# Gated layers: each head's mean of squares from high and low parts in the short format, the norm's steps two k-steps later

## The reference

```python
def rmsnorm(x, g):
    y = xf * lax.rsqrt(jnp.mean(xf * xf, axis=-1, keepdims=True) + EPS)
    return y * g
# gla_mixer: q, k, v, r from h @ w_in; o from the chunked recurrence
# y = (rmsnorm(o, head_norm) * silu(r)) @ w_out
```

## Time and profile before

| | us |
|---|---|
| median of 3 runs | 2536.77 (2536.25 to 2537.08) |
| the profiled execution | 2536.17 |
| its span | 2534.4 |
| PE busy | 2516.1 (99%) |
| DVE busy | 1747.4 (69%) |
| ACT busy | 1206.0 (48%) |
| POOL busy | 169.1 (7%) |

### The profile page before, as it was taken

How to read it: one execution, slowest core, us unless ns; L and a number is a source line. 1 busy time by engine, 2 the same in 40 slices (tenths; PEclk the granted TensorE clock), 3 DMA queues, 4 the chain that set the end, 5 groups by cost and what they waited for, 6 DMA issues and landing times.

```text
span 2534.4 us, 48129 instructions
## 1 busy us (share of the span) xinstructions
PE 2516.1 (99%) x19925; PEld 2451.5 (97%) x19925; DVE 1747.4 (69%) x2578; ACT 1206.0 (48%) x1822; POOL 169.1 (7%) x180
## 2 busy tenths in 40 slices
PE   8999999999999999999999999999999999999998
PEld 8999999999988899999998899999999999999998
DVE  6555994984555599489557557948955565984973
ACT  5454651543555565245245545524534544642543
POOL 1101000001000010000122210000011101000001
PEclk9999999999999999999999999999999999999999
DMA  4222333332433233333222233332323223333332
GB/s 120 71 78 84 100 102 91 100 96 78 120 97 109 74 108 96 97 95 96 85 68 76 70 91 88 102 102 84 97 81 88 72 70 90 109 88 93 106 89 78
DMA packets 443890, 230.68 MB, mean 91 GB/s; under 512 B 17092, under 2 KB 440736, under 8 KB 443696
## 3 DMA queue, kind: packets, MB, share of 16 engines
q1 hardware_dynamic: 442048, 226.90, 31.2%
q10 hardware_dynamic: 1200, 0.59, 0.1%
q0 software_dynamic: 448, 0.45, 0.1%
HBM read 219.03 MB, written 8.87 MB: 90 GB/s over the span
## 4 chain that ended last, share of the span: by engine, by line
PE 96%; DVE 2%; ACT 1%; issue 1%; DMA 0%; SPq 0%; ACTq 0%; DVEq 0%
PE slot L2378 32%; PE slot L2421 21%; PE aux L2885 6%; PE aux L2880 6%; PE aux L2882 6%; PE slot L2885 5%; PE slot L2880 5%; PE slot L2882 5%; PE aux L2337 2%; PE aux L2783 1%; PE aux L2546 1%; PE aux L2789 1%; PE aux L2695 1%; PE aux L2633 1%; PE aux L2561 1%
## 5 line engine op out<-in xcount | busy, mean ns | idle before, releaser
L765 ACT ACTIVATE w_hi<-raw 128x1024 fp32r<-128x1024 f32 (+3 forms) x208 | 241.1, 1159 | 275.3 <-PE slot L2421 136.7
L2378 PE MATMUL slot<-xg_hi,w_hi 128*128 128x272 f32 x1664 | 361.4, 298 | 2.5 <-DVE w_lo L1462 1.5
L2378 PE MATMUL slot<-xg_lo,w_hi 128*128 128x272 f32 x1664 | 343.7, 288 | 0.0
L2378 PE MATMUL slot<-xg_hi,w_lo 128*128 128x272 f32 x1664 | 343.6, 288 | 0.0
L1462 DVE TENSOR_TENSOR w_lo<-raw,w_hi 128x1024 fp32r<-128x1024 f32 (+4 forms) x208 | 284.2, 1366 | 68.8 <-ACT w_hi L765 66.8
L2378 PEld LDWEIGHTS slot<-xg_hi,w_hi 128*128 128x128 f32 x1664 | 260.5, 189 | 14.2 <-issue 7.8
L2378 PEld LDWEIGHTS slot<-xg_lo,w_hi 128*128 128x128 f32 x1664 | 261.3, 188 | 0.0
L2378 PEld LDWEIGHTS slot<-xg_hi,w_lo 128*128 128x128 f32 x1664 | 260.3, 189 | 0.0
L2982 POOL TENSOR_TENSOR sq_sum<-sq_sum,sq_x 128x544 f32<-128x544 f32 x48 | 67.9, 1414 | 1609.8 <-ACT sq_x L783 1609.5
L2097 DVE TENSOR_TENSOR ffn_y<-slot,rstd 128x544 f32<-128x544 f32 x56 | 40.6, 725 | 193.9 <-PE slot L2421 177.7
L2421 PE MATMUL slot<-h_hi,w_hi 128*128 128x272 f32 x1078 | 150.0, 287 | 0.0
(11 more groups left out here) (406 smaller groups left out, 5757.4 us busy)
## 6 DMA issues: line engine op xcount, KB each, us to landing
raw<-in_l_ffn_w_out_dram SPq DMA_DIRECT2D x64, 704.0 KB, 4.7
raw<-in_l_ffn_w_in_dram SPq DMA_DIRECT2D x52, 512.0 KB, 5.0
raw<-in_l_gla_w_in_dram SPq DMA_DIRECT2D x47, 512.0 KB, 3.9
ffn_raw_b<-in_l_ffn_w_in_dram SPq DMA_DIRECT2D x88, 256.0 KB, 3.4
ffn_raw_b<-in_l_ffn_w_in_dram SPq DMA_DIRECT2D x44, 512.0 KB, 5.2
raw<-in_l_ffn_w_in_dram SPq DMA_DIRECT2D x72, 256.0 KB, 3.4
raw<-in_l_att_w_qkv_dram SPq DMA_DIRECT2D x24, 512.0 KB, 3.8
raw<-in_l_lru_w_in_dram SPq DMA_DIRECT2D x24, 512.0 KB, 3.9
```

The source lines that it names most:

```text
L765: act.activation(w_hi[par][:, 0:kt, :], raw[par][:, 0:kt, :], ACT.Copy).then_inc(s_hi, 1)
L2378: ins = pe.matmul((slot[par] if bank is None else bank)[:, hf, 0:HALF], w[par][:, k, :], a[:, k0 + k, hf * HALF:(hf + 1) * HALF], start=(k ...
```

## The change

- The sum of squares is split as the weights are: ACT copies it to fp32r (`square_hi`, step 64), DVE subtracts the copy from it (`square_lo`, step 65). The two parts lie where `inv` and `sq1` lie.
- The mean is four fp32r matmuls with a constant matrix of 1/256 in fp32r, which the format holds exactly: 512 columns and 32 columns of the high part, then the same of the low part, summed in PSUM. PE waits for the low part.
- The mean moves from step 66 to 68, the root from 67 to 69, the inverse from 69 to 71, the norm products from 70 and 71 to 72 and 73.
- The constant is written by DVE into a start-up tile and copied once to fp32r by ACT at the start.
- Some semaphores are merged (abs and exp share one, cumulative sum and middle share one); the waits and their order stay.

```diff
-        mean_h = sb("mean_h", [P, P])
+        mean_hr = sb("mean_h", [P, P], F32R)
...
             act.wait_ge(s_vk, 3)
+            act.activation(mean_hr[:, :], ST["mean_f"][:, :], ACT.Copy)
             act.activation(rms5[:, 0:1], eps[:, 0:1], ACT.Sqrt)
...
+                def square_hi(h):
+
+                    q = h + 4 * gl
+                    act.wait_ge(s_hp, q + 1)
+                    act.wait_ge(s_on, 2 * q)
+                    act.activation(GL["sq_hi"][:, :], GL["sq0"][:, :], ACT.Copy).then_inc(s_sqh, 1)
...
-                    if n == 67:
+                    if n == 64:
+                        square_hi(h)
+                    if n == 69:
                         head_rms(h)
...
+                def square_lo(h):
+
+                    q = h + 4 * gl
+                    dve.wait_ge(s_sqh, q + 1)
+                    dve.tensor_tensor(GL["sq_lo"][:, :], GL["sq0"][:, :], GL["sq_hi"][:, :].bitcast(F32),
+                                      ALU.subtract).then_inc(s_sql, 1)
...
-                    if n == 69:
+                    if n == 65:
+                        square_lo(h)
+                    if n == 71:
                         head_inv(h)
-                    if n in (70, 71):
-                        o_norm(h, n - 70)
+                    if n in (72, 73):
+                        o_norm(h, n - 72)
...
                 def mean_sq(h):
 
-                    pe.wait_ge(s_hp, h + 4 * gl + 1)
-                    pe.matmul(A0[:, :], mean_h[:, :], GL["sq0"][:, 0:SEQ], start=True, stop=True)
-                    pe.matmul(A1[:, 0:DEC_SEQ], mean_h[:, :], GL["sq0"][:, SEQ:TOK], start=True, stop=True).then_inc(s_hst, 1)
+                    pe.wait_ge(s_sql, h + 4 * gl + 1)
+                    for part, src in enumerate((GL["sq_hi"], GL["sq_lo"])):
+                        pe.matmul(A0[:, :], mean_hr[:, :], src[:, 0:SEQ], start=(part == 0), stop=(part == 1))
+                        ins = pe.matmul(A1[:, 0:DEC_SEQ], mean_hr[:, :], src[:, SEQ:TOK], start=(part == 0), stop=(part == 1))
+                    ins.then_inc(s_hst, 1)
...
-                    if n == 66:
+                    if n == 68:
                         mean_sq(h)
```

More of the change, by code:

```diff
@@ L243, in make_start @@
                         tri_f=a("tri_f", [P, P]), behind=a("start_behind_gate", [P, 48 * P]), gain_rows=a("gain_rows", [P, P]),
-                        squares=a("x_rows_sq", [P, QT + 1, D_MODEL]), xs=a("x_sample_gain", [P, XT, DEC_SEQ]))
+                        squares=a("x_rows_sq", [P, QT + 1, D_MODEL]), xs=a("x_sample_gain", [P, XT, DEC_SEQ]),
+                        mean_f=a("mean_f", [P, P]))
         def make_ffn(a):
@@ L259, in make_gla @@
         def make_gla(a):
+            with ExitStack() as c:
+                sb("gla_in_front", [P, 11 * TOK], F32, c)
+                sq_hi = sb("gla_sq_hi", [P, TOK], F32R, c)
+                sb("gla_sq0_there", [P, TOK], F32, c)
+                sq_lo = sb("gla_sq_lo", [P, TOK], F32R, c)
             b = {n: a("gla_" + n, [P, TOK]) for n in
                  ("q", "k", "z", "mn", "ez", "b", "eb", "enb", "ekd", "ke", "kd", "inv", "sq0", "sq1")}
-            b["yv"] = b["q"]
+            b["yv"], b["sq_hi"], b["sq_lo"] = b["q"], sq_hi, sq_lo
             b["wb_in"], b["low_in"] = b["sq0"][0:GATE_ROWS, 0:GLA_HEADS * GLA_DK], b["sq1"][0:GATE_ROWS, :]
@@ L334, in encoder_step @@
         s_raw = [sem(f"raw_in{s}") for s in range(2)]
-        s_mid, s_bm = sem("gla_mid"), sem("gla_b_from_mid")
+        s_bm = sem("gla_b_from_mid")
         s_hi, s_lo, s_mm, s_free = sem("w_hi"), sem("w_lo"), sem("block_done"), sem("block_read")
@@ L342, in encoder_step @@
         s_out7, s_dcp, s_tact, s_tdve, s_xd = sem("seven_summed"), sem("seven_d_b_copied"), sem("t_act"), sem("t_dve"), sem("x_from_scaled")
-        s_wb, s_gm, s_z, s_abs, s_exp, s_ln, s_mn, s_g, s_b, s_e, s_df, s_ekd = (sem("gla_" + n) for n in (
-            "gate_b_in", "gate_mm", "z", "abs", "exp", "ln", "min", "g", "cumsum", "exps", "diff", "exp_kd"))
+        s_wb, s_gm, s_z, s_ez, s_ln, s_mn, s_g, s_b, s_e, s_df, s_ekd = (sem("gla_" + n) for n in (
+            "gate_b_in", "gate_mm", "z", "abs_then_exp", "ln", "min", "g", "cumsum_then_mid", "exps", "diff", "exp_kd"))
         s_qe, s_ke, s_kd, s_vtm, s_vte, s_kdm, s_kde, s_atm, s_ate, s_um, s_s, s_om, s_oe, s_sil = (sem("gla_" + n) for n in (
@@ L371, in encoder_step @@
             "mm", "x", "square", "x_gain", "squares_summed", "mean_mm", "rms", "inv_rms", "turned"))
-        s_hp = sem("head_square")
+        s_hp, s_sqh, s_sql = sem("head_square"), sem("head_square_hi"), sem("head_square_lo")
         def one3(t, n, a, b, parts=slice(0, P)):
@@ L861, in gate @@
                     act.wait_ge(s_g, q)
[L862 to L865, removed]
+                    act.activation(GL["ez"][:, :], GL["z"][:, :], ACT.Abs).then_inc(s_ez, 1)
+                    act.wait_ge(s_ez, 2 * q + 1)
+                    act.activation(GL["ez"][:, :], GL["ez"][:, :], ACT.Exp, scale=-1.0).then_inc(s_ez, 1)
+                    act.wait_ge(s_ez, 2 * q + 2)
                     act.activation(GL["ez"][:, :], GL["ez"][:, :], ACT.Ln, bias=1.0).then_inc(s_ln, 1)
@@ L1447, in _ @@
             dve.memset(row_sq[:, :], 1.0)
-            dve.memset(mean_h[:, :], 1.0 / GLA_DV)
+            dve.memset(ST["mean_f"][:, :], 1.0 / GLA_DV)
             dve.memset(chunk_go[:, :], 1.0).then_inc(s_vk, 1)
@@ L1630, in cumsum @@
                     dve.tensor_tensor_scan(GL["b"][:, :], chunk_go[:, :], GL["mn"][:, :], 0.0, ALU.mult, ALU.add).then_inc(s_b, 1)
-                    dve.wait_ge(s_b, q + 1)
+                    dve.wait_ge(s_b, 2 * q + 1)
                     spans = GL["b"][:, 0:SEQ].rearrange("p (c n) -> p c n", n=P)
@@ L1635, in cumsum @@
                     dve.tensor_tensor(b_end[:, 0:NCHUNK - 1], GL["b"][:, P - 1:SEQ - P:P], GL["b"][:, P + CHUNK - 1:SEQ:P],
-                                      ALU.add).then_inc(s_mid, 1)
-                    dve.wait_ge(s_mid, q + 1)
+                                      ALU.add).then_inc(s_b, 1)
+                    dve.wait_ge(s_b, 2 * q + 2)
                     dve.tensor_tensor(spans[:, :, 0:CHUNK], spans[:, :, 0:CHUNK],
```

## The result

The changed kernel takes 2539.78 us (median of 20 runs, 2538.01 to 2541.65) against 2536.46 for the kernel before on the same chips (20 runs, 2535.75 to 2537.13): a ratio of 1.0013, 95% interval 1.0007 to 1.0019. That is 3.3 us slower, within 0.2%. The profiled execution took 2539.79, its span is 2538.1. The runs of the changed kernel spread over 3.6 us, those of before over 1.4.

What follows compares the result with a forecast made beforehand. PE was taken as the bound, with 96% of the chain. Terms of −1.9 (mean), +0.3 (waits in heads 0 to 2) and +3.4 (head 3) gave +1.8 us on 2536.77: 2538.6, range 2534.2 to 2541.2.

Steps and rivals of the forecast that it cites:

- part 1: Mean's matmuls on PE: 0.68 us a head instead of 1.00, or 1.09 in head 3; 2.7 us gain if nothing waits.
- Rival E: Mean's matmuls: four weight loads lie open, 0.92 us a head, gain 0.08 instead of 0.32; 2540.0 us, chance 0.05.
- part 2: Squares' copy on ACT and subtract on DVE: 16 instructions, about 11 us, off the bounding engine; no cost.
- part 3: Heads 0 to 2, turning the next head's v waits for ACT's root: 0.05 us for each of six heads, 0.3 us.
- Rival D: Heads 0 to 2: turning v waits for a whole table load, up to 1.28 us a head; 2546.3 us, chance 0.05.
- part 4: Behind head 3: late root and inverse delay the low split, PE stalls 2.1 us; net cost 1.7 twice, 3.4 us.
- Rival C: Head 3's chain holds one more ACT table load of 1.28 us in each layer; 2541.2 us, chance 0.05.
- Rival B: Head 3's stall doesn't come and only the gain is left; 2534.3 us, chance 0.11.

Runs made afterwards that it cites:

- e4: The changed kernel with the mean itself done in plain float32 on the unsplit sum, all steps and waits kept; 2540.51 us.
- e2: The changed kernel with only head 3's norm products moved from steps 72 and 73 to 74 and 75, behind the low weight split; 2535.29 us.
- e6: The changed kernel with head 3's root at step 68 and inverse at 69, norm products left at 72 and 73; 2535.09 us.
- e8: The changed kernel with the squares' copy at step 65 and their subtract at 66, behind the weight splits; 2535.86 us.
- e1: The changed kernel with head 3's root at step 68, inverse at 69 and norm products at 74 and 75; 2533.84 us.
- e7: The changed kernel with each of head 3's two norm products done twice on DVE, to lengthen the stall; 2543.67 us.

## Why the prediction was right

2538.6 was forecast, in the range 2534.2 to 2541.2, with no change beyond 0.2% the likeliest; 2539.78 was measured. Of the 3.3 us by which the change is slower the sum had 1.8. On the runs in which the clock held (2538.0 to 2538.5, median 2538.2) the change costs +1.7 against 2536.46, and the sum had said +1.8. The mechanism was right as far as it went. That the number is only 1.2 us off owes something to luck: the fall of the clock (1.6 in the median run) was not foreseen, and the kernel before came out at 2536.46 and not at the 2536.77 that the forecast was built on, which hid 0.3 of it. The range held by the room left for other reasons, and three of the twenty runs lie above it (2541.24 to 2541.65).

- **The PE time of the mean** (part 1): 0.68 forecast, 0.69 measured. Its inside was different. Behind the first narrow matmul the next one starts after 0.03 us, not 0.104; the second narrow one starts 0.31 behind its wide one instead of 0.23, 0.04 after the end of its weight load (187.46 + 0.19); and the last term holds the 0.09 by which the first pair of the k-step behind is longer. That these came to what I had put in by one estimate is partly chance. Rival E, with its loads in the open, falls: it had 0.92 for what took 0.69, and e4 measured the gain.
- **The squares' two steps** (part 2): copy 0.66, subtract 0.72, in the queues where they were expected. PE never waited for them.
- **Heads 0 to 2** (part 3): 0.05 a head was charged for the root, 0.09 was paid in heads 0 and 1 (0.27 in place of 0.18 between sample scores and transposes). Moving the mean away from the transposes also cost something that the sum didn't name: the k-step behind it has a long first pair, and the one behind v's transposes keeps its own (85.83 to 86.16, 0.33). This 0.09 is inside the measured 0.69. Rival D, a whole table load there, falls: the load ran 82.28 to 83.56, ahead of the mean's end at 84.40.
- **Head 3** (part 4): the stall of 2.1 us was forecast and is 2.0, in both layers, at the block I had named. On the way there each link is within 0.1 us of the trace, when it is counted from the slot read (184.07 in the rows, 183.56 in the changed kernel): inverse 7.84 forecast (191.91 − 184.07), 7.82 measured (191.38 − 183.56); low split done 14.55 (198.62 − 184.07) and 14.48. e2, e6 and e8 each took a link out of the way and got back what it held.
- **What was missing**: the clock. I carried durations over "as they stand", since before had 1.00 in every slice, but a stall of 2 us is just what before didn't have. In the median run one fall is paid, 1.6 us: 2538.2 + 1.6 = 2539.8. The term that failed is thus one that the sum didn't have, and it is as large as the sum's whole result.
- Rival C's number, 2541.2, came nearer than it deserved: its extra table load isn't in the trace. The load ends at 189.19 + 1.28 = 190.47 and the root starts at 190.49, so nothing of 1.38 us stands between them. The Trainium skill (ScalarE: Activation LUTs, What ACT_TABLE_LOAD costs) adds a drain of that length to every switch of tables; this trace doesn't show it.
- Rival B, the gain alone, was priced at 2534.3. e1 is that case: 2533.84.

## What to carry to other kernels

A step moved by a fixed number lands between different neighbours in different rounds of a loop: look at the round whose neighbours differ (here the last head, with silu, y_hi and the low split around it) and follow the queue link by link, in order, until the next thing that the bounding engine waits for. The two k-steps cost 0.09 us a head in three heads and cost the whole gain and more in the fourth, and giving that one its own numbers was worth 5.9 us. When a sum predicts an idle time on TensorE where there was none, the clock behind it needs a term of its own.

## What the runs showed of the hardware

- Behind an idle time of TensorE of 1.85 us (recorded), the granted clock fell to the 1.2 GHz level in about half of the cases: 19 in 40, counted from the three groups of run times (20 runs, two layers). Behind 1.46 us the 11 runs of e4 show none, behind 3.2 us every run of e7 shows at least one. I had taken two microseconds within 2500 of full work to be too little to matter.
- The fallen stretch lasted 3.4 us in each of the three that were profiled, but it began at different places: 0.4 us after the engine had resumed (changed kernel, layer 0), 1.1 to 1.3 after (e7, layer 3), and in e7's layer 0 already 0.55 before, inside the idle time. It costs 1.4 to 1.6 us, and 1.4 is the one of which a part fell into the idle time.
- The first pair of a k-step took 0.33 to 0.34 us in place of 0.25 behind each group of short matmuls looked at: the float32 mean (187.12 to 187.46 before, and e4), the fp32r mean (187.72 to 188.06) and the transposes (85.83 to 86.16). Behind a wait of 1.85 us it took 0.35 (198.09 to 198.44), the same as behind 3.23 (2098.63 to 2098.98 in e7, at the full clock). A group of its own between k-steps pays this once more than one that stands beside another.
